# Attention bias by distance: a store to HBM from 128 partitions, read back in 16 skewed transfers

## The reference, cut to what matters

```
q, k: 4 heads, 512 tokens; block i holds the queries i*128 .. i*128+127
bias[h, q, k]  = rel_bias[t5_bucket(k - q), h]      # rel_bias: 32 buckets x 4 heads
s              = (q . k) * 48**-0.5 + bias
p              = softmax(where(k//64 <= q//64, s, -inf))
```

## Time and profile before

| | before |
|---|---|
| time, median of 3 runs (lowest, highest) | 1065.41 us (1064.02, 1067.14) |
| span of the profiled execution, core 0 | 1065.3 us |
| TensorE busy | 1016.7 us (95%) |
| VectorE, ScalarE, GpSimd busy | 504.8, 353.6, 85.1 us |
| mean granted TensorE clock | 0.977 |
| data moved by DMA | 95.86 MB |
| of it, on GpSimd's queue (q0) | 3.38 MB |

### The profile page before, as it was taken

The page is one execution under the profiler, slowest core; times in us unless marked ns, Lnnn a source line. Parts: engine busy times, 40 slices in busy tenths (PEclk is TensorE's granted clock), DMA queues, the critical chain, the costliest instruction groups (busy, mean ns, idle before and its releaser), DMA issues. The chain is left out here.

```text
span 1065.3 us, 13344 instructions
## 1 busy us (share of the span) xinstructions
PE 1016.7 (95%) x5044; PEld 835.3 (78%) x5044; DVE 504.8 (47%) x719; ACT 353.6 (33%) x475; POOL 85.1 (8%) x75
## 2 busy tenths in 40 slices
PE   7955999999999999999989999999999999999996
PEld 5844888888888888877889788788888888888886
DVE  6421444444434434377673885544444444423324
ACT  4412344444322212345644233232322333323221
POOL 6000000000002213000020102400000000000002
PEclk8987999999999999999999999999999999999998
DMA  5233322222322234211221122222222222332212
GB/s 182 68 64 79 102 95 90 91 98 98 121 94 97 81 103 121 104 60 60 67 62 52 50 64 96 98 79 99 98 98 98 95 89 94 119 108 83 96 67 79
DMA packets 28226, 95.86 MB, mean 90 GB/s; under 512 B 4369, under 2 KB 6545, under 8 KB 28193
## 3 DMA queue, kind: packets, MB, share of 16 engines
q1 hardware_dynamic: 26384, 92.01, 25.8%
q0 software_dynamic: 1664, 3.38, 1.8%
q10 hardware_dynamic: 144, 0.02, 0.0%
HBM read 91.98 MB, written 3.41 MB: 90 GB/s over the span
## 5 line engine op out<-in xcount | busy, mean ns | idle before, releaser
L379 PE MATMUL ps<-xg_hi,w_hi 128*128 128x512 f32 x848 | 338.7, 399 | 32.2 <-DVE w_lo L1056 28.1
L772 ACT ACTIVATE w_hi<-raw 128x1024 fp32r<-128x1024 f32 (+2 forms) x155 | 174.7, 1127 | 489.1 <-PE ps L381 450.6
L380 PE MATMUL ps<-xg_lo,w_hi 128*128 128x512 f32 x848 | 333.7, 393 | 0.0
L381 PE MATMUL ps<-xg_hi,w_lo 128*128 128x512 f32 x848 | 333.2, 393 | 0.0
L1056 DVE TENSOR_TENSOR w_lo<-raw,w_hi 128x1024 fp32r<-128x1024 f32 (+2 forms) x155 | 208.2, 1343 | 227.6 <-ACT w_hi L772 227.4
L379 PEld LDWEIGHTS ps<-xg_hi,w_hi 128*128 128x128 f32 x848 | 161.2, 190 | 78.2 <-DVE w_lo L1056 29.5
L381 PEld LDWEIGHTS ps<-xg_hi,w_lo 128*128 128x128 f32 x848 | 161.2, 190 | 34.6
L380 PEld LDWEIGHTS ps<-xg_lo,w_hi 128*128 128x128 f32 x848 | 161.5, 190 | 32.3
L379 PE MATMUL ps<-h_hi,w_hi 128*128 128x512 f32 (+1 forms) x374 | 143.3, 383 | 0.0
L380 PE MATMUL ps<-h_lo,w_hi 128*128 128x512 f32 (+1 forms) x374 | 143.1, 383 | 0.0
L381 PE MATMUL ps<-h_hi,w_lo 128*128 128x512 f32 (+1 forms) x374 | 143.1, 383 | 0.0
(11 more groups left out here) (171 smaller groups left out, 810.6 us busy)
## 6 DMA issues: line engine op xcount, KB each, us to landing
raw<-up_w SPq DMA_DIRECT2D x88, 512.0 KB, 3.2
raw<-down_w SPq DMA_DIRECT2D x32, 704.0 KB, 4.0
raw<-t_w SPq DMA_DIRECT2D x18, 512.0 KB, 3.3
raw<-out_w SPq DMA_DIRECT2D x8, 512.0 KB, 3.3
raw<-nat_w SPq DMA_DIRECT2D x6, 576.0 KB, 3.8
x<-xT SPq DMA_DIRECT2D x8, 256.0 KB, 4.9
out<-x SPq DMA_DIRECT2D x8, 256.0 KB, 2.3
bias_by_distance<-dv POOLq DMA_DIRECT2D x1, 1280.0 KB, 56.5
```

Source lines behind the costliest of these rows:

```text
L379: pe.matmul(out_ap, a[0], b[0], start=first, stop=False)
L380: pe.matmul(out_ap, a[0], b[1], start=False, stop=False)
L381: return pe.matmul(out_ap, a[1], b[0], start=False, stop=last)
L772: act.activation(w_hi[:, slot(s), 0:w], raw[:, slot(s), 0:w], ACT.Copy).then_inc(hi_ready, 1)
```

## The change

`rel_bias` is handed over with each head's column repeated 32 times, so `relb` is 32 x 128 and the product has 128 rows: partition 32h+c holds a copy of the vector of head h. VectorE copies all 128 partitions. The store writes those 128 rows once, without a repeating source: 128 x 640 values. HBM then holds 32 copies for each head where there were 128, so one skewed read can fill only 32 partitions, and each head is read in four DMAs, each starting 32 elements earlier than the one before: 16 DMAs in all. VectorE waits for 16 of them.

```diff
+COPIES = P // HEADS
-    tvec = nc.dram_tensor("bias_by_distance", (HEADS, P, 5 * P), F32, kind="Internal")
+    tvec = nc.dram_tensor("bias_by_distance", (HEADS * COPIES, 5 * P), F32, kind="Internal")
-        relb = sb("relb", [32, HEADS])
+        relb = sb("relb", [32, P])
-        tv_s = dv[0:HEADS].rearrange("h b f -> h (b f)")[:, 0:5 * P]
+        tv_s = dv[:].rearrange("p b f -> p (b f)")[:, 0:5 * P]
-            pool.dma_start(tvec.ap(), tv_s[:, None, :].to_broadcast([HEADS, P, 5 * P])).then_inc(bias_stored, 16)
+            pool.dma_start(tvec.ap(), tv_s).then_inc(bias_stored, 16)
             for h in range(HEADS):
-                rows = bass.AP(tvec, h * P * 5 * P + P - 1, [[5 * P - 1, P], [1, S]])
-                pool.dma_start(dbias[:, h, :], rows).then_inc(bias_loaded, 16)
+                for g in range(HEADS):
+                    rows = bass.AP(tvec, h * COPIES * 5 * P + P - 1 - g * COPIES, [[5 * P - 1, COPIES], [1, S]])
+                    pool.dma_start(dbias[g * COPIES:(g + 1) * COPIES, h, :], rows).then_inc(bias_loaded, 16)
-                    last = pe.matmul(ps[0:HEADS, 5 + lo // S, 0:hi - lo], relb[:], onehot_s[:, lo:hi],
+                    last = pe.matmul(ps[:, 5 + lo // S, 0:hi - lo], relb[:], onehot_s[:, lo:hi],
-                    last = dve.tensor_scalar(tv_s[:, lo:hi], ps[0:HEADS, 5 + lo // S, 0:hi - lo], DK ** 0.5, None,
+                    last = dve.tensor_scalar(tv_s[:, lo:hi], ps[:, 5 + lo // S, 0:hi - lo], DK ** 0.5, None,
-                dve.wait_ge(bias_loaded, 16 * HEADS)
+                dve.wait_ge(bias_loaded, 16 * HEADS * HEADS)
-        "rel_bias": a["rel_bias"],
+        "rel_bias": np.repeat(a["rel_bias"], COPIES, axis=1),
```

## The result

| | before | after |
|---|---|---|
| time, median of four runs each | 1065.63 us | 1035.28 us (1034.81 to 1036.32) |
| ratio, 95% interval | | 0.9714 (0.9703 to 0.9725) |
| span of the profiled execution | 1065.3 us | 1034.5 us |
| TensorE busy | 1016.7 us (95%) | 1010.6 us (98%) |
| on GpSimd's queue (q0) | 3.38 MB | 2.39 MB |

The change makes the kernel faster by 30.4 us. The prediction was 1036.3 us.

The account below looks back on a forecast made before the run. TensorE's matmuls bound the kernel, with time lost in the first SwiGLU block to loads held up by the bias store. 1065.3 - 29.4 + 0.3 = 1036.2 us of span, so 1036.3 us; range 1033.5 to 1041.

Parts of the forecast that it names:

- What bounds the kernel: First SwiGLU block, 53 to 107 us: TensorE stood 24.7 us in two waits, traced back through VectorE and ScalarE to late loads.
- Why the store holds up the loads: Bias store from four partitions holds four engines, 0.86 us a packet, 55 us; slab loads' shares on those engines wait.
- The loss, 29.4 us: Between gate products at 49.31 and 111.39 us: 24.6 us of TensorE waits plus 4.8 us of slow matmuls.
- The store: Bias store of 0.33 MB from 128 partitions: taken as 5 us, upper bound 14.1 us, cost 0 over the whole bound.
- The product: Bias matmul with 128 weight columns in place of 4: +0.3 us on TensorE, between 0 and 0.4.
- VectorE's copy: Copy of the product from PSUM, 128 rows in place of 4: cost 0, as VectorE is idle 1.08 us behind it.
- The reads: Sixteen bias reads on GpSimd's queue from 418.9 us: 0.54 us an issue, 5.0 us to land, 10 us early, cost 0.
- A: Bias reads back are served one after another: sixteen take 59 us, total 1069.7 us; chance 2 in 100.
- B: Store is not what holds up the loads, or the new one does as much: 1065.6 us; chance 2 in 100.
- C: Part of the loss stays at the store, a wait of 1 to 5 us: 1037.5 to 1041.5 us; chance 10 in 100.
- D: Clock not granted as before in steady work without the two rests: 1047 to 1057 us; chance 2 in 100.
- The sum: Whole kernel: 1065.3 - 29.4 + 0.3 = 1036.2 us of span; median 0.1 above the span, so 1036.3 us.

Follow-up runs that it names:

- runs with 64 and 32 copies: Kernel before, its four-partition store repeating each row 64 or 32 times instead of 128, with 8 or 16 reads: ratio 0.9858 (1051.59 us) and 0.9730 (1038.1 us).
- all copies from 128 partitions: Kernel after, but its store writes each of 128 rows 4 times (1.31 MB) and four reads replace the sixteen: ratio 0.9712, 1035.42 us.
- partitions 0, 36, 72, 108: Kernel after's product and copy, store from only these four partitions, each row 128 times (1.31 MB), four reads: ratio 0.9713, 1035.03 us.
- sixteen reads alone: Kernel before with its own store, but sixteen reads of the bias in place of four: ratio 0.9998.
- run with 32 copies: Kernel before, store still from four partitions but each row repeated 32 times instead of 128 (0.33 MB), sixteen reads: ratio 0.9730, 1038.1 us.

## Why the prediction was right

**What bounds the kernel** held: the chain from TensorE's wait through VectorE and ScalarE to the loads, and from there to the store, was the loss. Taking the store from other partitions brings the whole of it with the 1.31 MB and the four reads of before (all copies from 128 partitions; partitions 0, 36, 72, 108), and the reads bring nothing (sixteen reads alone). That the slow store is what delays the loads follows from the runs with 64 and 32 copies: its length is cut, and the waits go one after the other.

**Why the store holds up the loads** held in part. That four engines were held and the loads' shares waited on them agrees with the runs with 64 and 32 copies. But the prediction took the 0.86 us of a packet as it stood. It is no property of an engine: 16 engines on single partitions move 28 GB/s where four engines on four neighbours move 23, and four engines on rows further apart are three times as fast.

**The loss, 29.4 us,** was 62.08 - 32.64 = 29.44. Both parts of it went: TensorE's two waits, and with them the lower clock, the stretch being at 1.00 throughout.

**The store** was put at 5 us with bounds of 2.3 and 14.1 at no cost. It took 2.6, nearly what the nearest row written to HBM took. The upper bound was not free: a store of 15.0 us from four neighbours makes TensorE wait 1.4 us. The forecast did not need it, but the argument that this term is 0 over the whole bound was wrong in two places, as the run with 32 copies shows.

**The product** was put at +0.3 us. From the gate product ahead of it to the one behind it, 41.24 to 49.38 us after and 41.29 to 49.31 before, it cost 0.12. All profiles of kernels with a product of 4 rows have 8.02 or 8.03 us there, all with 128 rows 8.13 or 8.14.

**VectorE's copy** took 0.82 us in its two instructions where it took 0.81, and cost nothing. **The reads** were put at 0.54 us an issue and 5 us to land at no cost; they took 0.50 and 2.0 to 3.9, and cost nothing. The estimate of 0.36 us from a slope per row failed: the issue does not go by rows alone, since the store of 512 rows was issued in 1.25 us from four partitions and in 0.85 from 128.

**The rivals.** A is out by the sixteen reads alone. B is out by every run that moved the store's source rows. C did not come: no wait of TensorE is left between 45 and 110 us. Nor did D: the one new slice at eight tenths of the clock, the 21st, is a stretch of the mixer that was as slow before (a clock of 0.87 and 22.16 us busy in 26 us, from 517 us after and from 547 before) and now falls within one slice.

**The sum** left out one term: 1.2 us that came from the place of the tiles behind `relb`. It also took the span for 0.1 us under the time of its own execution. It is 1.8 us under it: after, the profiled execution took 1036.32 us with a span of 1034.5, and it is the longest of the four runs; by the same 1.8 us the span of 1065.3 belongs to the run of 1067.14, the longest of before. This did no harm, because the forecast in effect starts from the median. The median of before with -29.44, +0.12 and -1.2 gives 1065.63 - 30.52 = 1035.1 us; measured 1035.28. So the forecast of 1036.3 was 1.0 us high, most of it the term left out, and its own margin covered that.

The two profiles lie 30.8 us apart, 0.3 more than these terms. The mixer, from the last update of `x` in the first down projection to the first in the out projection, took 235.29 us before and 234.85 after. But the same stretch is anywhere from 233.69 to 236.38 us in the thirteen profiles, so a difference of this size there says nothing about the change.

## What to carry to other kernels

A DMA that repeats a few neighbouring partitions is slow out of proportion to its bytes, and it held back the slab loads, which have a share on its engines: look in the profile for a DMA share stuck at a simple fraction (here a quarter) while loads that elsewhere take 3 us take 25. Give such a transfer source rows on many partitions, as 128 copies from a wider matmul cost 0.12 us here, and don't cut it into pieces of one partition (0.85% slower here). When a change moves a tile's size, compare the pace of untouched stages too; here a shift of the tiles behind it was worth a microsecond.

## What was not expected of the hardware

**Sixteen engines get hardly more out of single partitions than four engines out of four neighbours.** 16 engines, 96.5% of their time taken by the store, moved 28 GB/s of it, four moved 23, and 128 source partitions gave 247 GB/s.

**Where the tiles start matters to TensorE's pace.** With `h_hi` and all behind it at a multiple of 64 bytes (addresses from the kernels' allocation) a tile of the down projection takes 15.40 us, at a multiple of only 32 it takes 15.46, 0.4% more; in the out projection, which reads `mixed_hi` and `mixed_lo` there, it is 5.60 and 5.62. The upward projections, whose operand `xg_hi` starts at the same place in all kernels (32896, a multiple of 64), kept their 10.88 us for two slabs throughout. The pad shifts every tile behind `relb`; that it is the matmul's operand that counts is read from which stages changed, and was not tried tile by tile.

**The start of the kernel differs by 1.2 to 1.9 us between executions of equal work.** The store was issued at 48.2 to 48.6 us in some executions and at 46.7 to 47.0 in others, whichever the kernel. The stretch from 20 to 40 us in the profiles of before and of the sixteen reads alone:

```profile
20.00:40.00 20.00, 18.75 (x83) 15.26 (x84) 8.48 (x12) 4.78 (x6) 3.02 (x2) 0.91 0.23 79
```

```profile
20.00:40.00 20.00, 18.74 (x89) 15.44 (x90) 9.38 (x14) 6.27 (x8) 3.10 (x2) 1.00 0.24 79
```

The granted clock was 0.91 in the one and 1.00 in the other, and TensorE got through 83 and 89 matmuls in the same busy time. In both TensorE stood idle just before 22.1 us, for 1.25 and 1.26 us, with the clock at 1.00. In before the clock then read 0.50, the level of 1.2 GHz, between 23 and 25 us; in the other it stayed at 1.00. Why one execution dropped and the other did not stays open. That is why spans of single profiles are compared stage by stage here.
